# Two transformer blocks on one core: attention values a step later, the forget gate's log moved, and ScalarE's order in the first layer

## The reference

```python
# first block: two layers, each modulated by a condition vector c
m = silu(cond) @ w_ada[layer] + b_ada[layer]          # shift, scale, gate: 3 x 1024
x = rms_norm(h, norm_w) * (1 + scale) + shift
# layer 0: spatial gating (layer_norm, gelu, w_s) beside differential attention, 4 heads
# layer 1: latent attention, 8 heads
h = h + gate * (mix @ w_out)

# second block: two hybrid layers (w_in: 1024 x 10832)
oa = causal softmax attention                                   # rotary, 8 heads
oc = causal softmax attention with logit += sum(log_sigmoid(f)) # "forget", no rotary
ob = softmax attention over the 64 best keys of an index score  # rotary, 8 index heads
y  = sum over branches of sigmoid(merge) * ((o * silu(g)) @ w_branch)
h  = h + y @ w_out
```

## Time and profile before

| | |
|---|---|
| median of 3 runs | 1097.83 us (1097.78 to 1099.08) |
| the profiled execution | 1097.09 us, of it 1095.3 us span |
| TensorE busy | 1068.6 us, 98% of the span |
| VectorE busy | 728.4 us, 67% |
| ScalarE busy | 598.5 us, 55% |
| 16 DMA engines, hardware queue | 51.3% of the span |
| read from HBM | 162.66 MB |

### The profile page before, as it was taken

How to read it: one execution, slowest core, us unless ns; L and a number is a source line. 1 busy time by engine, 2 the same in 40 slices (tenths; PEclk the granted TensorE clock), 3 DMA queues, 4 the chain that set the end, 5 groups by cost and what they waited for, 6 DMA issues and landing times.

```text
span 1095.3 us, 18406 instructions
## 1 busy us (share of the span) xinstructions
PE 1068.6 (98%) x6981; PEld 901.6 (82%) x6981; DVE 728.4 (67%) x1555; ACT 598.5 (55%) x1218; POOL 2.6 (0%) x10
## 2 busy tenths in 40 slices
PE   5999999999999999999999999999999999999997
PEld 3677777788897779988798988889978898888887
DVE  5534376666588766788578866657787678765564
ACT  4524334543355455566766774445576667664445
POOL 0000000000000000000000000000000000000000
PEclk9999999999999999999999999999999999999999
DMA  9997461122332224554555455666464445556662
GB/s 311 324 307 230 137 218 41 56 59 77 96 102 82 77 59 117 158 154 116 155 146 143 140 169 175 191 192 182 133 167 133 131 142 155 154 156 192 191 183 67
DMA packets 215710, 164.90 MB, mean 151 GB/s; under 512 B 7092, under 2 KB 189096, under 8 KB 215624
## 3 DMA queue, kind: packets, MB, share of 16 engines
q1 hardware_dynamic: 215088, 162.75, 51.3%
q0 software_dynamic: 192, 0.66, 0.2%
q10 hardware_dynamic: 344, 0.32, 0.1%
HBM read 162.66 MB, written 1.05 MB: 149 GB/s over the span
## 4 chain that ended last, share of the span: by engine, by line
PE 82%; DVE 9%; ACT 4%; issue 2%; SPq 2%; DMA 1%; DVEq 0%; ACTq 0%
PE pj L1978 23%; PE pj L1980 21%; PE pj L1979 21%; DVE w_lo L1282 3%; PE tr L2513 1%; PE ac L2317 1%; ACT w_hi L808 1%; PE sc L2158 1%; PE tr L2165 1%; SPq L739 1%; PE ac L2452 1%; PE sc L2303 1%; PE ac L2179 1%; PE pj L2072 1%; DMA ada_raw<-in_ada_w_dram 1%
## 5 line engine op out<-in xcount | busy, mean ns | idle before, releaser
L1282 DVE TENSOR_TENSOR w_lo<-raw,w_hi 128x1024 fp32r<-128x1024 f32 (+2 forms) x258 | 309.4, 1202 | 177.8 <-ACT w_hi L808 177.2
L1978 PE MATMUL pj<-h_hi,w_hi 128*128 128x256 f32 (+1 forms) x1088 | 345.6, 318 | 3.1 <-DVE h_lo L1356 0.9
L1980 PE MATMUL pj<-h_hi,w_lo 128*128 128x256 f32 (+1 forms) x1088 | 334.0, 307 | 0.0
L1979 PE MATMUL pj<-h_lo,w_hi 128*128 128x256 f32 (+1 forms) x1088 | 333.9, 307 | 0.0
L808 ACT ACTIVATE w_hi<-raw 128x1024 fp32r<-128x1024 f32 (+2 forms) x258 | 267.9, 1040 | 101.8 <-PE pj L1980 99.5
L1978 PEld LDWEIGHTS pj<-h_hi,w_hi 128*128 128x128 f32 x1088 | 207.7, 191 | 33.4 <-issue 20.6
L1980 PEld LDWEIGHTS pj<-h_hi,w_lo 128*128 128x128 f32 x1088 | 207.9, 191 | 10.1
L1979 PEld LDWEIGHTS pj<-h_lo,w_hi 128*128 128x128 f32 x1088 | 208.1, 191 | 8.2
L1978 PE MATMUL pj<-w_hi,h_hi 128*128 128x512 f32 x288 | 114.7, 398 | 0.0
L1979 PE MATMUL pj<-w_lo,h_hi 128*128 128x512 f32 x288 | 112.3, 390 | 0.0
L1980 PE MATMUL pj<-w_hi,h_lo 128*128 128x512 f32 x288 | 112.2, 390 | 0.0
(11 more groups left out here) (336 smaller groups left out, 1428.4 us busy)
## 6 DMA issues: line engine op xcount, KB each, us to landing
raw<-in_w_in_dram SPq DMA_DIRECT2D x152, 512.0 KB, 3.7
ada_raw<-in_ada_w_dram SPq DMA_DIRECT2D x48, 512.0 KB, 7.6
raw<-in_even_w_in_dram SPq DMA_DIRECT2D x28, 512.0 KB, 4.9
raw<-in_w_branch_dram SPq DMA_DIRECT2D x24, 512.0 KB, 3.6
raw<-in_w_out_dram SPq DMA_DIRECT2D x16, 512.0 KB, 4.0
raw<-in_odd_w_in_dram SPq DMA_DIRECT2D x11, 512.0 KB, 4.0
raw<-in_even_w_out_dram SPq DMA_DIRECT2D x8, 512.0 KB, 3.9
raw<-in_odd_w_out_dram SPq DMA_DIRECT2D x8, 512.0 KB, 4.2
```

Of the source, the lines that this page charges most:

```text
L1282: last = nc.vector.tensor_tensor(lo, src, hi.bitcast(F32), ALU.subtract)
L1978: nc.tensor.matmul(dst, lh, rh, start=first, stop=False)
L1979: nc.tensor.matmul(dst, lh, rl, start=False, stop=False)
L1980: return nc.tensor.matmul(dst, ll, rh, start=False, stop=final)
```

## The change

It does five things. (1) In layer 0 of the first block ScalarE empties the chunk's bank first, and copies the turned `av`, `bv` and `ws` tiles after it. (2) `condition_turn` uses two transposes of 128 columns in place of two matmuls with `pick2`; VectorE's `ada_finish` adds the four row groups by a reduction from PSUM and then the bias, and `pick2` is gone. (3) In the hybrid layers pair 0 stays at step 10 and every other pair comes a step earlier, at 9 + 4t; values keep their steps 12 + 4t, by a table of their own. (4) Index scores move to steps 12, 15, 19, 23, the second rotation to step 18, and the selection rounds by up to three steps. (5) The forget gate's log moves from step 10 to 18 and gets an Exp on a constant behind it, its rows from step 11 to 20, the cumulative sums from step 12 to 21 and their split from 13 to 22.

```diff
@@ tables
-PAIR_SLOT = {10 + 4 * t: t for t in range(NTRIP)}
-IDX_SLOT = {13: 0, 16: 1, 20: 2, 24: 3}
-KI_SLOT, QI_SLOT = 4, {11: 0, 17: 1}
-TOPK_SLOTS = (25, 27, 28, 31, 33, 35, 39, 40)
-DECAY_SLOT = 12
-FEW_SLOT = 9
+PAIR_SLOT = {9 + 4 * t + (t == 0): t for t in range(NTRIP)}
+VALUE_SLOT = {12 + 4 * t: t for t in range(NTRIP)}
+IDX_SLOT = {12: 0, 15: 1, 19: 2, 23: 3}
+KI_SLOT, QI_SLOT = 4, {11: 0, 18: 1}
+TOPK_SLOTS = (24, 27, 28, 30, 31, 35, 38, 39)
+FEW_SLOT, LOG_SLOT, ROWS_SLOT, DECAY_SLOT = 9, 18, 20, 21
+VALUE_TURNS = ("av", "bv", "ws")
@@ ScalarE, first block, layer 0
-                while TURNS1[n_turn][0] == s - 1 and TR1[n_turn][0] not in L1_TURNS:
+                while TURNS1[n_turn][0] == s - 1 and TR1[n_turn][0] not in (*L1_TURNS, *VALUE_TURNS):
                     l0_turned(n_turn)
                     n_turn += 1
...
                 elif 3 <= s <= L0_IN:
                     l0_evacuate(s - 1)
+                while TURNS1[n_turn][0] == s - 1 and TR1[n_turn][0] in VALUE_TURNS:
+                    l0_turned(n_turn)
+                    n_turn += 1
@@ ScalarE, hybrid layer
-                    t = PAIR_SLOT.get(s - 3)
+                    t = VALUE_SLOT.get(s - 1)
...
-                    if s == FEW_SLOT + 1:
+                    if s == LOG_SLOT:
                         act.wait_ge(fx_set, lay + 1)
                         after(nc.scalar.activation(lfa, lf, ACT.Abs))
                         after(nc.scalar.activation(lfa, lfa, ACT.Exp, scale=-1.0))
                         nc.scalar.activation(lfa, lfa, ACT.Ln, bias=ones[:, 0:1]).then_inc(fe_set, 1)
+                        nc.scalar.activation(small[:, 61:62], ones[:, 0:1], ACT.Exp)
@@ VectorE
-            nc.vector.tensor_reduce(pick2[:], ident.rearrange("p (c a) -> p a c", c=4)[:, 0:2, :], AX_X, ALU.add)\
-                .then_inc(cond_zero, 1)
...
-                nc.vector.tensor_tensor(mod[:, layer, m0:m0 + 2, :], ada_bank(n)[1][:, 0:4].rearrange("p (e a) -> p e a", e=2),
-                                        bias, ALU.add).then_inc(signal, 1)
+                parts = ada_bank(n)[1][:, 0:2 * P].rearrange("p (e c q) -> p e q c", e=2, c=4)[:, :, 0:2, :]
+                after(nc.vector.tensor_reduce(mod[:, layer, m0:m0 + 2, :], parts, AX_X, ALU.add))
+                nc.vector.tensor_tensor(mod[:, layer, m0:m0 + 2, :], mod[:, layer, m0:m0 + 2, :], bias, ALU.add)\
+                    .then_inc(signal, 1)
...
-                    if s == FEW_SLOT + 2:
+                    if s == ROWS_SLOT:
@@ TensorE
-                    last = nc.tensor.matmul(ada_bank(n)[1][:, 2 * e:2 * e + 2], ada_rows[:, n % 2, P * e:P * e + P], pick2[:],
-                                            start=True, stop=True)
+                    last = nc.tensor.transpose(ada_bank(n)[1][:, P * e:P * e + P], ada_rows[:, n % 2, P * e:P * e + P], ident)
...
-                    if s - 2 in PAIR_SLOT:
-                        pair_values(PAIR_SLOT[s - 2])
+                    if s in VALUE_SLOT:
+                        pair_values(VALUE_SLOT[s])
```

More of the change, by code:

```diff
@@ L434, in build_program @@
         cond = sb("cond", [P, KT, 2])
-        pick2 = sb("pick2", [P, 2])
         scr = sb("scr", [P, 2, TOK])
@@ L1396, in _ @@
             dve.wait_ge(ident_in, 16)
-            nc.vector.tensor_reduce(pick2[:], ident.rearrange("p (c a) -> p a c", c=4)[:, 0:2, :], AX_X, ALU.add)\
-                .then_inc(cond_zero, 1)
             token_squares()
             dve.wait_ge(cond_t, 1)
-            dve.wait_ge(cond_zero, 2)
+            dve.wait_ge(cond_zero, 1)
             after(nc.vector.scalar_tensor_tensor(cond[:].rearrange("p k a -> p a k"), cond[:].rearrange("p k a -> p a k"), 1.0,
```

## The result

| | before | changed |
|---|---|---|
| median of the runs compared | 1097.92 us (4 runs) | 1083.66 us (4 runs, 1082.26 to 1084.47) |
| profiled execution | 1097.09 us, span 1095.3 | 1083.43 us, span 1081.6 |
| mean granted clock of the profiled one | 0.997 | 0.996 |

The ratio is 0.9867 with a 95% interval of 0.9849 to 0.9884: 14.3 us faster, where the forecast was 10.8. That is the low end of the range (1083.5): the median lies 0.2 us inside it, and the ratio times the median that the forecast started from (1097.83) gives 1083.2, 0.3 us outside. The direction and nearly all the places were right; the size was 3.5 us short.

A forecast was written before the change was run, and what follows sets the result against it. TensorE, busy for 98% of the span, was taken as the bound. Terms of 1.5 + 1.6 + 3.7 + 4.0 = 10.8 us off 1097.09 gave 1086.3, plus 0.74 for the median: forecast 1087.0 us, range 1083.5 to 1092.8.

The forecast's parts named there:

- B: Condition's modulation turns, two transposes for two pick matmuls: 1.6 us saved, bounds 0.5 and 3.3.
- the hand count of C: VectorE and ScalarE followed through hybrid steps 10 to 22: pair 3 late, 0.5 us of new wait per layer.
- C: Hybrid layers, steps 10 to 20: waits of TensorE removed, less new ones, 3.7 us gained net.
- A: First layer, five places: ScalarE empties the chunk's bank earlier, TensorE's wait goes; 1.5 us, bounds 0 and 1.7.
- B, sixteen turns of the steps: Turns after the opening: 1.5 us saved, 0.17 each ahead of transposes, nothing ahead of attention values.
- B, opening: Opening's eight turns wait for ScalarE's copies and weights; only the last can gain, 0.1 us.
- C, waits removed: Waits at steps 10, 12 and 19 of the hybrid layers go: 2.54 and 2.15 us, together 4.7 us.
- C, new waits: Wait at pair 3's transposes behind the moved log: 0.5 us per hybrid layer, 1.0 us to pay; bounds 0 and 5.6.
- D: Hybrid layers: values and next scores side by side, two excursions from the projections become one; 4.0 us, bounds 0 and 4.4.
- D, joints: Eleven joints of values with the next scores per hybrid layer, each saving 0.20 us.
- D, cumulative sums alone: Cumulative sums of the hybrid layers, before beside values in step 12, now stand alone and cost 0.20 us per layer.
- The rival of a late VectorE: ScalarE's moved log makes VectorE late in steps 20 to 22, 2.8 us more wait per hybrid layer: 1092.6 us; chance 0.12.

The follow-up runs named there:

- e6: Changed kernel with the logarithm, forget-gate rows and cumulative sums back at steps 10, 11 and 12; median 1088.58 us, ratio to before 0.9907.
- e9: Changed kernel with logarithm, rows and cumulative sums back at steps 10 to 12, no dummy Exp, values back two steps behind their scores; median 1091.62 us, ratio 0.9952.
- e1: Changed kernel with pick matmuls and the old VectorE addition in all 24 condition turns; median 1085.01 us, ratio to before 0.9887.
- e3: Kernel before with transposes in the opening's eight condition turns alone; median 1097.03 us, ratio to before 0.9996.
- e12: Kernel before with transposes in all 24 condition turns; median 1095.10 us, ratio to before 0.9982.
- e2: Changed kernel with pick matmuls in the opening's eight condition turns, transposes in the other sixteen; median 1083.93 us, ratio to before 0.9873.
- e4: Kernel before with ScalarE's order alone, emptying the value chunk's bank ahead of the transposed tile; median 1097.39 us, ratio to before 0.9994.

## Why the prediction fell short

The mechanisms of the prediction held. What failed are three steps of its sum: B's price for a turn (1.3 us too little), the hand count of C that charged new waits (1.0 us that nobody pays), and the later pairs of C, taken as moved without effect (0.9 us missed).

With the clock alike in both (one low stretch near 450 us and the one at the end, none in the opening) the changed kernel is 14.6 us ahead: 13.7, and the 0.9 us by which e6, with the same opening and no low stretch in it, is through it earlier (1.1 in e9). Against the terms of the sum:

| term | forecast | runs |
|---|---|---|
| A | 1.5 | 1.5 |
| B, sixteen turns of the steps | 1.5 | 2.8 |
| B, opening | 0.1 | 0.1 (up to 0.4 in other executions) |
| C, waits removed | 4.7 | gone, all of them |
| C, new waits | -1.0 | 0.0 |
| waits on VectorE's bank near the last pair | not seen | 0.9 |
| D, joints | 4.4 | 4.3 |
| D, cumulative sums alone | -0.4 | 0.0 |

**A was right** in place and in size. What I had late instead, the copy of the turned tile by 0.6 us, isn't late at all: it starts 0.67 us after the first transpose in before (59.14 to 59.81 in the earlier trace rows) and 0.63 after it in the changed kernel (59.79 to 60.42). ScalarE had stood idle until the transposes were through, and empties the bank in that time.

**B's direction was right and its term mis-sized.** Two choices did it. For the five turns ahead of attention values I set the price of leaving transposes (0.17 us), read at fp32 matmuls of another shape, against a pick turn of 0.36 us and got nothing; 0.22 us is saved, 0.14 in the turn itself. And I compared only the time from the turn's start to that of its follower. Ahead of attention values the pick turn also makes the group behind it 0.08 us longer, as the eight values show; the `condition` matmuls take 1.00 us behind either. The four turns ahead of `condition` and fp32 scores save 0.12 and not 0.07, the one ahead of a projection 0.23 and not 0.18. The six ahead of transposes save 0.17, as forecast. VectorE's reduction, for which no row stood, took 0.17 us and its addition 0.16, 0.21 us apart: hidden in the steps, as said.

**C: the waits went; the failing step is the hand count of what is late instead.** It charged 0.5 us per layer. With P the start of pair 2's scores in step 17 (506.43), the changed kernel's ScalarE, beside the earlier trace rows, and TensorE's next transposes:

```profile
512.48 0.20 ACT L1213 ACTIVATE work<-work 128x16 f32<-128x16 f32 x1
...
512.95 1.28 ACT L1215 ACT_TABLE_LOAD   x1
...
514.57 1.28 ACT L1216 ACT_TABLE_LOAD   x1
515.86 0.20 ACT L1216 ACTIVATE small<-ones 128x1 f32<-128x1 f32 x1
...
517.92 0.88 ACT L1227 ACTIVATE tanh<-sc 128x384 f32<-128x384 f32 x2
...
525.79 1.19 ACT L1243 ACTIVATE expd<-expd,small 128x256 f32<-128x256 f32 x3
...
528.64 0.82 PE L2516 MATMUL tr<-const,expd 128*128 128x128 f32 x6
```

The logarithm starts at P + 6.05 (count: P + 7), the dummy Exp is out at P + 9.6 (P + 10.8), the relus at P + 12.4 (P + 14), pair 3's scores are read at P + 16.6 (P + 18.5), its probabilities are out at P + 20.5 (P + 22.4). TensorE comes at P + 22.2, as counted. So the count ran 1 us late at its start and 1.9 at its end, and its zero of slack was 1.7 us. The doubled loads bear this out: 2.9 us more on ScalarE, 1.1 to 1.3 of wait. The rival of a late VectorE (5.6 us of wait over both layers) needed everything 2.8 us later than the count; everything was 1.0 to 1.9 us earlier.

On that rival's rule page and runs differ. Both switches of tables in step 18 take 1.28 us, and the next operation on ScalarE begins 0.01 us behind each (by the starts shown and the Ln at 514.24); the 2.66 us with drain that the Trainium skill (ScalarE: Activation LUTs, What ACT_TABLE_LOAD costs) gives are not seen in this kernel.

**The 0.9 us not seen** were in the trace of before: a wait of the projection on the bank that VectorE empties, 0.20 us by the list of waits, at 650 and 968 us:

```profile
650.14 0.28 PE L1980 MATMUL pj<-h_hi,w_lo 128*128 128x256 f32 x1
650.62 0.36 PE L1978 MATMUL pj<-h_hi,w_hi 128*128 128x256 f32 x1 [0.20 <-DVE work L1785]
```

By starts it is 0.48 us less 0.12, and 0.07 more at the second matmul: 0.43. I followed steps 10 to 22 and took the later pairs as moved without effect. In before VectorE does pair 11's mask and minimum (from 647.40) right ahead of emptying this bank (from 649.79); with pair 11 at step 53 that work lies a step earlier, and no wait shows in the changed kernel or in e9.

**D was right** to 0.1 us in its joints; the charge for the lone cumulative sums was wrong by 0.4.

Together 1.3 + 1.0 + 0.9 + 0.3 (D) = 3.5 us of the 3.8 between 10.8 and 14.6; 0.3 us are not placed. The misses have one sign: three costs that the trace did not show (leaving transposes, the new waits, the lone cumulative sums) I took near their dear end, and the fourth miss is a gain that I did not look for.

## What to carry to other kernels

Compare what a group costs together with the group behind it, up to the second matmul of the main stream: part of what a group costs can be paid by its follower (here 0.08 us of the 0.22). A hand count of two engines over ten steps drifts by a microsecond or two; give such a count that much room on both sides, and don't let it charge a wait by itself. When two things are moved up together, ask whether the one runs into what had held up the other: here the index scores alone would have met the logarithm. When an order is moved as a whole, read its far end as well as the steps in which the edit is: the list of waits had 0.20 us where the starts had 0.43. And before a difference of 1 us is given to an edit, look at the granted clock of both traces at 1 us resolution.

## What the hardware showed that I had not expected

**The granted clock fell for 3.4 or 6.8 us, and not at the same places in each execution.** The mean clock of all four executions of the changed kernel is 0.994 or 0.996, of before 0.993 to 0.998. Apart from the end of the span, where every one of the traces has 4.4 us or more of it, the low level (1.2 GHz) stands in stretches of 3.4 or 6.8 us. At the border to the hybrid layers, near 450 us, nine of the traces have it and four have not, with the same instructions around it. The window of the changed kernel is shown above; this is the kernel with pick matmuls everywhere, in the same four windows:

```profile
31.40:34.80 3.40, 1.82 (x24) 1.00 1.10 348
34.80:38.20 3.40, 3.40 (x17) 1.00 1.11 346
444.10:447.50 3.40, 3.16 (x28) 1.00 0.84 227
447.50:450.90 3.40, 3.40 (x31) 1.00 0.21 64
```

What the engine did before was alike (busy 3.15 and 3.16 of 3.4 us), the outcome was not. Missing it gives back 1.5 us in e1, e3, e6 and e9; an extra one near 230 us costs 1.55 to 1.6 (e12, e2, e4). In the opening, where weights are waited for anyway, one of 3.4 us at 34.8 us costs 0.9 to 1.0 and one at 23 us nothing. What decides is open. Both kernels with the early logarithm fell to the low level near 487 us, right behind 1.8 and 1.7 us of waits, and before, with 0.8 us of such waits at this place, did not; but e9 had the same 1.7 us of waits in its second layer and kept its clock there, where e6 did not. It was not tested further.

The Trainium skill (TensorE: Matmul & The Clock Gate, Part 4: PE-mode transpose) says that a transpose does not count as a busy TensorE in the same way as a matmul. As a reason for the stretch at 34.8 us the traces give it no support, and they are too few to speak against it: the low clock of the opening came in three of five executions with pick matmuls, 6.8 us each time, and in six of eight with transposes, 3.4 us each time.
